# Attention results transposed by VectorE in 32x32 blocks and DMA moves, in place of TensorE's transposes

## The chip, the cores and the metric

One core of a Trainium2 chip runs the whole program. Its engines run side by side, each through its own instruction queue in order: TensorE (PE; its weight loads are listed as PEld), VectorE (DVE), ScalarE (ACT), GpSimd (POOL) and SyncE (SP), which only issues DMAs. They meet through semaphores. The metric is the device time of one launch in microseconds; the difference that a measurement of this kernel can tell is small, since its three runs lie within 0.15 us.

## The reference, cut to what matters

Two layers of a decoder trunk, for 256 tokens of 1024 channels in float32. In each layer a token mixer with three branches (latent attention, a convolution module, a pooling mixer) is merged by gates, and a gated feed-forward network follows. The change touches the attention branch between the weighted values and the output projection:

```
def mla_branch(...):
    ...
    def attend(args):
        qn, qr, start = args
        s = jnp.einsum('bqhd,bkhd->bhqk', qn, k_nope) + jnp.einsum('bqhr,bkr->bhqk', qr, k_rope)
        ...
        p = jax.nn.softmax(s, axis=-1).astype(v.dtype)
        return jnp.einsum('bhqk,bkhd->bqhd', p, v)
    o = lax.map(attend, (qn_blocks, qr_blocks, starts))
    o = o.transpose(1, 0, 2, 3, 4).reshape(B, S, N_HEADS * V_HEAD_DIM)
    return o @ w_o
...
merged = gates[:, :, 0] * y_attn + gates[:, :, 1] * y_conv + gates[:, :, 2] * y_pool
return rms_norm(merged @ w_mix_o, norm_post)
```

Here `o` is 256 tokens by 512 channels (8 heads of 64). For `o @ w_o` TensorE wants `o` with the channels on the partitions: four tiles of 128 channels by 256 tokens.

## The kernel before

**Matrix products in three parts.** Every large product is made of three matmuls: each operand is split into a rounded high part and a low part (the rest), and high x high, high x low and low x high are summed (L460 to L462). Weights stream in as 135 units of 128 x 1024 for each layer. For each unit SP issues the load into a ring of five buffers (L398), ACT makes the high part (`hi`, L861), DVE the low part (`lo`, L1182 where the unit has a scale for its rows, L1186 where not), and TensorE uses it for 12 matmuls of 512 columns. SP may load unit g + 5 when the low part of unit g is done, and ACT makes a high part when TensorE has finished with the unit five earlier. So ACT and DVE work up to four units ahead of TensorE.

**The gate phase.** Units 25 to 48 of a layer (`U_GATE`; here gate 0 to gate 23) are the products for the three sigmoid gates. Between them TensorE does attention, by hand-written order: after gate i, for even i, `after_gate` gives step n = i/2 - 1 of scores, n - 1 of transposed probabilities (P) and n - 2 of weighted values (V). A step is two heads and one half of the tokens, so V0 to V7 follow gates 6 to 20, and V3 completes the first four heads, V7 the last four. ACT and DVE go through the same list with their own parts: while they stand at gate i they split the weights of gate i + 4. In each gate DVE also runs four taps of the convolution (L1261) until all 124 are done, in gate 19.

**The results of attention.** `divide` (L1401) reads V from the PSUM bank and writes the normalised result into `o_sb`. Then, at gates 20 and 22 (`O_AFTER`), `o_transposes` (L748) has TensorE transpose half the channels of `o_sb` each time, four transposes of 128 x 128 through L534 into a `tp` bank (uses O0 and O1 of the bank list `TP`). ACT copies the bank into `hT_hi` (`hi_T`, L895), DVE makes the rest, `hT_lo` (`lo_T`, L1214).

**The convolution's norm** runs beside it, across four engines: the last tap lets GpSimd sum the tiles (L1646 and L1648, the first sum), TensorE forms the mean after gate 22 (L756), DVE centres (L1349), ACT squares (L1024), GpSimd sums again (the second sum), TensorE forms the variance (L782, ahead of unit 51), DVE reads it (`conv_var`, L1357), GpSimd takes the root (L1657), DVE makes a diagonal (L1360), and TensorE spreads it (L788, ahead of unit 52).

**After the gates** come the output projections: pooling (units 49 to 52), attention (`U_ATTNO`, units 53 to 56), convolution (57 to 60). Only the attention units read the transposed results. The bands `sg` and `qk_flat` are reused by several stages: `sg` holds `pooled` until gate 2 and the squares `sq` from gate 23 on.

**A DMA pattern that exists already**: queries, keys and the hidden tiles of the feed-forward network are transposed by DVE in blocks of 32 x 32 (L1321, L1500), and DMAs then carry whole rows of blocks to the right partitions (GpSimd's queue at L1639 and L360, SP's at L360 and L425).

Of the kernel before, what the change touches and what calls it, by code (L numbers as in the profile page):

```python
# [86 lines left out]
def fulls(pair, use):  # L87
# [5 lines left out]
TP = (["X0", "X1", "X2", "X3", "HC0", "HC1", "CQ0", "CQ1", "CKV0", "CKV1",  # L93
       "MT0", "MT1", *(f"{piece}{n}" for n in range(8) for piece in "PV"), "O0", "O1",
       "M0", "M1", "M2", "M3", "F0", "F1", "F2", "F3"])
# [37 lines left out]

O_AFTER = (20, 22)
MT_AFTER, MEAN_AFTER = 2, 22
# [14 lines left out]
def build(nc, W, pool_w, par_d, const_d, gain_d, x_d, xc_d, pos_d, out_d):  # L150
    with ExitStack() as ctx:
# [3 lines left out]
        def sem(name):  # L155
            return ctx.enter_context(nc.semaphore(name))
# [53 lines left out]
        turned_k = [gates[:, 0, D:D + 512], gates[:, 1, D:D + 512], gates[:, 0, D + 512:2 * D]]  # L210
        placed_q = [qk_flat[:, 512 * i:512 * (i + 1)] for i in range(QUADS - 1)] + [gates[:, 1, 512:1024]]
        rope_a, rope_b = hc[:, 0, :], hc[:, 1, :]
        xc = hc[:, :, :].rearrange("p t n -> p (t n)").rearrange("p (c n) -> p c n", c=CT)
# [69 lines left out]
        q_stored = sem("q_stored")  # L283
        k_in = [sem(f"k_in{i}") for i in range(2)]
        conv_dve = sem("conv_dve")
        csum_done = sem("csum_done")
# [20 lines left out]
        def tokens(t):  # L307
            return slice(t * P, (t + 1) * P)
# [44 lines left out]
        def move_keys(eng, l, part):  # L353

            for h in range(2):
                eng.wait_ge(misc_full[h], l * 2 + 1)
            for i in range(HEAD_MOVES // 2 * part, HEAD_MOVES // 2 * (part + 1)):
                c, q = divmod(i, QUADS)
                eng.wait_ge(k_turned, l * (QK // BLK) + c + 1)
                eng.dma_start(u_hc[BLK * c:BLK * (c + 1), q // 2, q % 2, :], turned_k[c][BLK * q:BLK * (q + 1), :]  # L360
                              ).then_inc(k_in[part], 16)

        def hi_stored(eng, l, n):
# [20 lines left out]
        def _(sp):  # L384
# [42 lines left out]
            for l in range(LAYERS):  # L427
                for u in range(0 if l else 1, UNITS):
# [12 lines left out]
                    if u == U_GATE + 5:  # L441
                        move_keys(sp, l, 1)
                    if u == U_CQ:
                        load_gain(l, 0)
# [12 lines left out]
        def _(pe):  # L457
# [23 lines left out]
            for l in range(LAYERS):  # L481
# [265 lines left out]

                def o_transposes(half):  # L748
                    tp_emptied(pe, l, TPN[f"V{4 * half + 3}"])
                    transposes(TPN[f"O{half}"], [(o_sb[:, t, c * P:(c + 1) * P], P)  # L750
                                                 for c in range(2 * half, 2 * half + 2) for t in range(TOK)])

                def norm_mean():
# [5 lines left out]
                def attention(i):  # L759
# [5 lines left out]
                    if v_n is not None:  # L765
                        weighted_values(v_n)
                    if i in O_AFTER:
                        o_transposes(O_AFTER.index(i))
                    if i == MT_AFTER:
# [39 lines left out]
                col_group(U_POOLO + 2, 2, 2, 512, 1, "POOLO", HT, kt0=H_POOL, beside=norm_beside)  # L809
                for half in range(2):  # L810
                    tp_emptied(pe, l, TPN[f"O{half}"])
                col_group(U_ATTNO, 2, 2, 512, 0, "ATTNO", HT, kt0=H_O)
                col_group(U_ATTNO + 2, 2, 2, 512, 1, "ATTNO", HT, kt0=H_O)
# [31 lines left out]
        def _(act):  # L845
# [3 lines left out]
            for l in range(LAYERS):  # L849
# [185 lines left out]
                def store_p(m):  # L1035
# [3 lines left out]
                    if m >= 2:  # L1039
# [3 lines left out]
                                   ACT.Copy).then_inc(tp_free[n % 2], 1)  # L1043

                def exponentials(n):

# [8 lines left out]
                for i in range(GATES):  # L1055
# [20 lines left out]
                    if s_n is not None:  # L1076
                        exponentials(s_n)
                    if i in O_AFTER:
                        half_ = O_AFTER.index(i)
                        hi_T(f"O{half_}", hT_hi[:, H_O + 2 * half_:H_O + 2 * half_ + 2, :])  # L1080
                    if i == MT_AFTER:
                        for h in range(2):
                            hi_T(f"MT{h}", hT_hi[:, H_POOL + 2 * h:H_POOL + 2 * h + 2, :])
                    if i == 18:
                        act.preload_act_table(ACT.Silu)
                his(53, 56)
                conv_silu()
# [59 lines left out]
        def _(dve):  # L1147
# [23 lines left out]
            for l in range(LAYERS):  # L1171
# [223 lines left out]
                def divide(m):  # L1395
# [8 lines left out]
                                      ALU.mult).then_inc(tp_free[n % 2], 1)  # L1404

                for i in range(GATES):
                    s_n, p_n, v_n = after_gate(i)
# [4 lines left out]
                    if v_n is not None:  # L1412
                        divide(v_n)
                    if i == MEAN_AFTER + 1:
                        conv_centre()
                    lo(U_GATE + 4 + i)
                    if i == MT_AFTER:
                        for h in range(2):
                            k = slice(H_POOL + 2 * h, H_POOL + 2 * h + 2)
                            lo_T(f"MT{h}", hT_lo[:, k, :], hT_hi[:, k, :])  # L1420
                    if i in O_AFTER:
                        half_ = O_AFTER.index(i)
                        k = slice(H_O + 2 * half_, H_O + 2 * half_ + 2)
                        lo_T(f"O{half_}", hT_lo[:, k, :], hT_hi[:, k, :])
                    taps(4)
# [22 lines left out]

                los(53, 54)
                conv_var()  # L1450
                los(54, 55)
# [99 lines left out]
        def _(pool):  # L1551
# [30 lines left out]
            for l in range(LAYERS):  # L1582
# [54 lines left out]
                for c in range(QK // BLK):  # L1637
                    for q in range(QUADS):
                        pool.dma_start(placed_q[q][BLK * c:BLK * (c + 1), :], turned_q[c][BLK * q:BLK * (q + 1), :]  # L1639
                                       ).then_inc(q_in, 16)  # L1640
                move_keys(pool, l, 0)

                def tile_sum(src, which):
# [7 lines left out]
                pool.wait_ge(conv_dve, (l + 1) * len(TAP_ORDER))  # L1651
                tile_sum(cacc, 0)
                pool.wait_ge(sq_done, l + 1)
                pool.wait_ge(csum_done, l * 4 + 2)
# [131 lines left out]
```

## Time and profile before

| | us |
|---|---|
| median of 3 runs | 787.54 (787.43 to 787.58) |
| the profiled execution, its own time | 787.39 |
| its span, first to last instruction | 785.6 |
| TensorE busy | 777.3 (99%) |
| VectorE busy | 573.2 (73%) |
| ScalarE busy | 421.9 (54%) |
| GpSimd busy | 96.6 (12%) |

The busy share is an average. A matmul's duration is longer than the distance to the next one, since matmuls are pipelined: the 512-column ones take 0.39 us each and start 0.23 us apart. What a piece of TensorE's work costs is therefore read from starts, not from durations.

### The profile page before, as it was taken

How to read it: one execution, taken by the hardware profiler on the slowest of the kernel's cores; microseconds unless marked ns; L12 is line 12 of the kernel's file. 1: busy time of each engine (PE TensorE's matmuls, PEld its weight loads, DVE VectorE, ACT ScalarE, POOL GpSimd, SP SyncE). 2: the span in 40 equal slices, each digit the busy share in tenths (PEclk: the TensorE clock that was granted, in tenths of full speed). 3: DMA queues.
4: the chain of work that ended last, by engine and by line, in shares of the span. 5: the costliest groups of instructions: out<-in, count | busy, mean ns of one | idle time of the engine just before them, and what ended most of it. 6: DMA issues, size and time to landing. Idle time of an engine off the chain costs nothing.

```text
span 785.6 us, 10199 instructions
## 1 busy us (share of the span) xinstructions
PE 777.3 (99%) x3708; PEld 656.6 (84%) x3708; DVE 573.2 (73%) x826; ACT 421.9 (54%) x596; POOL 96.6 (12%) x147
## 2 busy tenths in 40 slices
PE   8999999999999999999999999999999999999997
PEld 7898888888888888888889888888888888888885
DVE  6689999789675666654476999996887665556553
ACT  6577555564554454454475656565546554445441
POOL 1624000122300000000221230002303000000000
PEclk9999999999999999999999999999999999999999
DMA  9677544545566666676365684444564666666631
GB/s 358 227 251 212 185 159 153 176 153 181 179 238 220 207 212 223 212 241 204 129 203 173 217 253 146 161 161 160 166 219 153 243 212 214 215 219 208 227 137 53
DMA packets 53456, 154.39 MB, mean 197 GB/s; under 512 B 10544, under 2 KB 15664, under 8 KB 53408
## 3 DMA queue, kind: packets, MB, share of 16 engines
q1 hardware_dynamic: 51856, 149.72, 57.3%
q0 software_dynamic: 1408, 3.52, 1.6%
q8 instruction: 29, 0.48, 0.3%
q10 hardware_dynamic: 144, 0.52, 0.2%
q14 instruction: 19, 0.16, 0.1%
HBM read 143.77 MB, written 1.05 MB: 184 GB/s over the span
## 4 chain that ended last, share of the span: by engine, by line
PE 98%; DMA 1%; ACT 0%; DVE 0%; DVEq 0%; POOLq 0%; issue 0%; POOL 0%; ACTq 0%
PE acc L460 28%; PE acc L462 28%; PE acc L461 28%; PE acc L579 7%; PE tp L534 2%; PE misc L725 1%; PE tp L743 1%; PE tp L546 1%; DMA gates<-x_cols 1%; PE misc L692 0%; PE tp L707 0%; PE misc L462 0%; PE misc L461 0%; PE misc L460 0%; PE misc L694 0%; ACT xT_hi L888 0%
## 5 line engine op out<-in xcount | busy, mean ns | idle before, releaser
L1186 DVE TENSOR_TENSOR w_lo<-raw,w_hi 128x1024 fp32r<-128x1024 f32 (+2 forms) x246 | 298.7, 1226 | 123.0 <-ACT w_hi L861 122.5
L861 ACT ACTIVATE w_hi<-raw 128x1024 fp32r<-128x1024 f32 (+2 forms) x252 | 258.1, 1039 | 163.2 <-PE acc L462 159.2
L460 PE MATMUL acc<-w_hi,xT_hi 128*128 128x512 f32 (+2 forms) x692 | 267.9, 387 | 0.0
L462 PE MATMUL acc<-w_hi,xT_lo 128*128 128x512 f32 (+2 forms) x692 | 264.9, 383 | 0.0
L461 PE MATMUL acc<-w_lo,xT_hi 128*128 128x512 f32 (+2 forms) x692 | 264.6, 382 | 0.0
L462 PEld LDWEIGHTS acc<-w_hi,xT_lo 128*128 128x128 f32 x692 | 129.9, 188 | 24.9
L461 PEld LDWEIGHTS acc<-w_lo,xT_hi 128*128 128x128 f32 x692 | 130.0, 188 | 24.0
L460 PEld LDWEIGHTS acc<-w_hi,xT_hi 128*128 128x128 f32 x692 | 130.0, 188 | 23.7
L460 PE MATMUL acc<-w_hi,hT_hi 128*128 128x512 f32 (+1 forms) x300 | 117.2, 391 | 0.0
L462 PE MATMUL acc<-w_hi,hT_lo 128*128 128x512 f32 (+1 forms) x300 | 116.2, 387 | 0.0
L461 PE MATMUL acc<-w_lo,hT_hi 128*128 128x512 f32 (+1 forms) x300 | 116.1, 387 | 0.0
L1261 DVE SCALAR_TENSOR_TENSOR cacc<-hcT,par,cacc 128x256 f32<-128x256 f32 x240 | 101.0, 479 | 0.0
L462 PEld LDWEIGHTS acc<-w_hi,hT_lo 128*128 128x128 f32 x300 | 56.3, 188 | 11.4
L461 PEld LDWEIGHTS acc<-w_lo,hT_hi 128*128 128x128 f32 x300 | 56.3, 188 | 11.1
L460 PEld LDWEIGHTS acc<-w_hi,hT_hi 128*128 128x128 f32 x300 | 56.3, 188 | 10.9
L1590 POOL TENSOR_SCALAR mean<-ssq 128x1 f32<-128x1 f32 x23 | 9.7, 422 | 442.9 <-ACT qk L880 442.4
L1050 ACT ACTIVATE qk<-misc,nmx 128x128 f32<-128x128 f32 (+1 forms) x32 | 13.2, 416 | 42.8 <-DVE nmx L1387 42.8
L1182 DVE SCALAR_TENSOR_TENSOR w_lo<-raw,par,w_hi 128x512 fp32r<-128x512 f32 (+1 forms) x30 | 25.4, 878 | 6.2 <-ACT w_hi L861 6.1
L1162 DVE TENSOR_TENSOR acc<-acc,gain 128x512 f32<-128x512 f32 x16 | 10.4, 691 | 25.6 <-ACT qk L880 22.6
L1507 DVE TENSOR_TENSOR hT_lo<-gates,hT_hi 128x512 fp32r<-128x512 f32 (+1 forms) x24 | 14.4, 639 | 20.1 <-ACT hT_hi L1102 20.1
L1102 ACT ACTIVATE hT_hi<-gates 128x512 fp32r<-128x512 f32 (+1 forms) x24 | 12.9, 586 | 24.9 <-DMA gates<-gates 24.8
L579 PE MATMUL acc<-w_hi,xT_hi 128*128 128x512 f32 x76 | 24.0, 396 | 1.5 <-ACT w_hi L861 1.5
(148 smaller groups left out, 640.9 us busy)
## 6 DMA issues: line engine op xcount, KB each, us to landing
raw<-weights SPq DMA_DIRECT2D x247, 512.0 KB, 3.8
raw<-weights SPq DMA_DIRECT2D x14, 384.0 KB, 3.4
gates<-gates SPq DMA_DIRECT2D x160, 32.0 KB, 2.5
raw<-weights SPq DMA_DIRECT2D x8, 288.0 KB, 3.7
gain<-gains SPq DMA_DIRECT2D x4, 512.0 KB, 7.0
qk<-gates POOLq DMA_DIRECT2D x18, 64.0 KB, 3.4
x_sb<-x_rows SPq DMA_DIRECT2D x2, 512.0 KB, 9.4
out_rows<-x_sb SPq DMA_DIRECT2D x4, 256.0 KB, 2.0
```

The lines of the kernel that those rows point to most:

```text
L460: pe.matmul(out, a_hi, b_hi, start=start, stop=False)
L461: pe.matmul(out, a_hi, b_lo, start=False, stop=False)
L462: return pe.matmul(out, a_lo, b_hi, start=False, stop=stop)
L534: mm = pe.transpose(tp[0:rows, b, i * P:(i + 1) * P], src, ident)
L579: mm = pe.matmul(b, src[:, kt, tokens(t)], w[:, s, 512 * j:512 * (j + 1)], start=kt == 0 and src is xT_hi and w is w_hi, stop=last and kt ...
L861: ins = act.activation(w_hi[:, s, first:end], raw[:, s, first:end], ACT.Copy, scale=by)
L1050: e = act.activation(probs[:, n % 2, i, 0:keys], misc[:, n % 2, i * keys:(i + 1) * keys], ACT.Exp, bias=nmx[:, n % 2, i:i + 1], accum_out= ...
L1102: act.activation(hid_part(hT_hi, j, t), placed_for(j, t), ACT.Copy).then_inc(hid_hi, 1)
L1182: ins = dve.scalar_tensor_tensor(out=w_lo[:, s, first:end], in0=raw[:, s, first:end], scalar=par[:, l, col:col + 1], in1=f(w_hi[:, s, firs ...
L1186: ins = dve.tensor_tensor(w_lo[:, s, 0:width], raw[:, s, 0:width], f(w_hi[:, s, 0:width]), ALU.subtract)
L1261: ins = dve.scalar_tensor_tensor(out=cacc[:, c, :], in0=src, scalar=w, in1=cacc[:, c, :], op0=ALU.mult, op1=ALU.add)
L1507: dve.tensor_tensor(hid_part(hT_lo, j, t), placed_for(j, t), f(hid_part(hT_hi, j, t)), ALU.subtract).then_inc(hid_lo, 1)
```

## The change

The two uses O0 and O1 of the transpose banks are gone, and with them four transposes each. In their place, for each half of the channels:

1. **DVE** turns the half in 32 x 32 blocks, two instructions of 128 x 256 (`turn_o`), after it has divided V3 (gate 12) and V7 (gate 20).
2. **DMAs** place the blocks, 16 for each half, each 32 partitions of 512 bytes (`move_o`). Half 0 goes by GpSimd's queue, behind the keys and ahead of the first sum. Of half 1, eight go by GpSimd's queue, between its first and its second sum, and eight by SP's, four behind the load of unit 54 and four behind the load of unit 55.
3. **ACT** makes the high part in two instructions of 128 x 256 (`hi_o`): of half 0 at gate 18, of half 1 behind the high part of unit 53.
4. **DVE** makes the low part likewise (`lo_o`): of half 0 at gate 18, of half 1 behind the low part of unit 53 and ahead of `conv_var`.
5. **TensorE** waits for the low parts ahead of units 53 and 54.

Half 0 lies in `sg`, half 1 in `qk_flat`.

```
-O_AFTER = (20, 22)
+O_TURNED, O_PARTS = (3, 7), 18
...
+        turned_o = sg[:, 0, :], qk_flat[:, 1024:1536]
+        placed_o = sg[:, 1, :], qk_flat[:, 0:512]
...
+        def move_o(eng, l, half, which, first, last):
+            eng.wait_ge(o_turned, TOK * (2 * l + half + 1))
+            for i in range(first, last):
+                a, q = divmod(i, QUADS)
+                eng.dma_start(placed_o[half][BLK * q:BLK * (q + 1), P * a:P * (a + 1)],
+                              turned_o[half][BLK * a:BLK * (a + 1), P * q:P * (q + 1)]).then_inc(o_in[which], 16)
...
+                    if U_ATTNO < u < U_ATTNO + 3:
+                        i = 8 + 4 * (u - U_ATTNO - 1)
+                        move_o(sp, l, 1, 1, i, i + 4)
...
-                def o_transposes(half):
-                    tp_emptied(pe, l, TPN[f"V{4 * half + 3}"])
-                    transposes(TPN[f"O{half}"], [(o_sb[:, t, c * P:(c + 1) * P], P)
-                                                 for c in range(2 * half, 2 * half + 2) for t in range(TOK)])
...
-                    if i in O_AFTER:
-                        o_transposes(O_AFTER.index(i))
...
-                for half in range(2):
-                    tp_emptied(pe, l, TPN[f"O{half}"])
-                col_group(U_ATTNO, 2, 2, 512, 0, "ATTNO", HT, kt0=H_O)
+                def results_ready(i):
+                    pe.wait_ge(o_lo, TOK * (2 * l + i + 1))
+                col_group(U_ATTNO, 2, 2, 512, 0, "ATTNO", HT, kt0=H_O, beside=results_ready)
...
+                def hi_o(half):
+                    o_landed(act, l, half)
+                    for t in range(TOK):
+                        act.activation(o_part(hT_hi, half, t), o_placed(half, t), ACT.Copy).then_inc(o_hi, 1)
...
-                his(53, 56)
+                his(53, 54)
+                hi_o(1)
+                his(54, 56)
...
+                def turn_o(half):
+                    tp_emptied(dve, l, TPN[f"V{O_TURNED[half]}"])
+                    v = o_sb[:, :, 2 * P * half:2 * P * (half + 1)]
+                    for t in range(TOK):
+                        dve.transpose(o_blocks(turned_o[half])[:, :, t, :, :].rearrange("p q k j -> p k q j"),
+                                      v[:, t, :].rearrange("p (k q j) -> p k q j", k=2, q=QUADS)
+                                      ).then_inc(o_turned, 1)
...
+                    if v_n in O_TURNED:
+                        turn_o(O_TURNED.index(v_n))
...
                 los(53, 54)
+                lo_o(1)
                 conv_var()
...
+                move_o(pool, l, 0, 0, 0, QUADS * QUADS)
...
                 tile_sum(cacc, 0)
+                move_o(pool, l, 1, 0, 0, QUADS * QUADS // 2)
                 pool.wait_ge(sq_done, l + 1)
```

How the instructions stand on TensorE around the end of gate 20, before (L743 is V7, L534 the transposes of O0, L460 the first matmul of gate 21):

```order
L462 MATMUL acc<-w_hi,xT_lo 128x512
L743 MATMUL tp<-v_sb,qk 128x64 [waits tp_free1,tp_free0]
L743 MATMUL tp<-v_sb,qk 128x64 x3
L534 MATMUL tp<-const,qk 128x128 [waits tp_free0,tp_free1]
L534 MATMUL tp<-const,qk 128x128 x3
L460 MATMUL acc<-w_hi,xT_hi 128x512 [waits lo_done]
```

and now (L780 is V7):

```order
L499 MATMUL acc<-w_hi,xT_lo 128x512
L780 MATMUL tp<-v_sb,qk 128x64 [waits tp_free1,tp_free0]
L780 MATMUL tp<-v_sb,qk 128x64 x3
L497 MATMUL acc<-w_hi,xT_hi 128x512 [waits lo_done]
L498 MATMUL acc<-w_lo,xT_hi 128x512
```

Between V7 and the next gate nothing is left. After gate 22 the same happens ahead of the convolution's mean.

GpSimd's queue between the keys and the root of the variance, before:

```order
L360 DMA u_hc<-gates 32x512 [waits k_turned] x5
L1646 TENSOR_TENSOR u_hc<-cacc 128x512 [waits conv_dve]
L1648 TENSOR_TENSOR u_hc<-u_hc 128x256 [waits csum_done]
L1646 TENSOR_TENSOR u_hc<-sg 128x512 [waits csum_done,sq_done]
L1648 TENSOR_TENSOR u_hc<-u_hc 128x256 [waits csum_done]
L1657 TENSOR_TENSOR crstd<-cvar,half 128x2 [waits var_in]
```

and now:

```order
L369 DMA u_hc<-gates 32x512 [waits k_turned] x5
L387 DMA sg<-sg 32x128 [waits o_turned]
L387 DMA sg<-sg 32x128 x15
L1702 TENSOR_TENSOR u_hc<-cacc 128x512 [waits conv_dve]
L1704 TENSOR_TENSOR u_hc<-u_hc 128x256 [waits csum_done]
L387 DMA qk<-qk 32x128 [waits o_turned]
L387 DMA qk<-qk 32x128 x7
L1702 TENSOR_TENSOR u_hc<-sg 128x512 [waits csum_done,sq_done]
L1704 TENSOR_TENSOR u_hc<-u_hc 128x256 [waits csum_done]
L1714 TENSOR_TENSOR crstd<-cvar,half 128x2 [waits var_in]
```

Eight DMAs stand now between the two sums, and sixteen ahead of the first.

VectorE from gate 19 on to `conv_var`, before (L1401 divides V7; the `hT_lo<-tp` rows are the low parts of O0 and O1):

```order
L1186 TENSOR_TENSOR w_lo<-raw,w_hi 128x1024 [waits hi_done]
L1261 SCALAR_TENSOR_TENSOR cacc<-hcT,par,cacc 128x256 [waits conv_dve] x3
L1401 TENSOR_TENSOR qk<-tp,rinv 128x128 [waits inv_done,tp_full1]
L1182 SCALAR_TENSOR_TENSOR w_lo<-raw,par,w_hi 128x512 [waits hi_done]
L1182 SCALAR_TENSOR_TENSOR w_lo<-raw,par,w_hi 128x512
L1214 TENSOR_TENSOR hT_lo<-tp,hT_hi 128x512 [waits tp_hi]
...
L1214 TENSOR_TENSOR hT_lo<-tp,hT_hi 128x512 [waits tp_hi]
L1349 TENSOR_TENSOR u_hc<-cacc,misc 128x1024 [waits misc_full0]
...
L1186 TENSOR_TENSOR w_lo<-raw,w_hi 128x1024 [waits hi_done]
L1357 TENSOR_SCALAR cvar<-misc 128x2 [waits misc_full1]
```

and now, from the low part of unit 47 at gate 18 on:

```order
L1224 TENSOR_TENSOR w_lo<-raw,w_hi 128x1024 [waits hi_done]
L1457 TENSOR_TENSOR hT_lo<-sg,hT_hi 128x2x128 [waits o_hi] x2
...
L1439 TENSOR_TENSOR qk<-tp,rinv 128x128 [waits inv_done,tp_full1]
L1449 STREAM_TRANSPOSE qk<-qk 128x2x4x32 [waits tp_free1]
L1449 STREAM_TRANSPOSE qk<-qk 128x2x4x32
...
L1387 TENSOR_TENSOR u_hc<-cacc,misc 128x1024 [waits misc_full0]
...
L1224 TENSOR_TENSOR w_lo<-raw,w_hi 128x1024 [waits hi_done]
L1457 TENSOR_TENSOR hT_lo<-qk,hT_hi 128x2x128 [waits o_hi] x2
L1395 TENSOR_SCALAR cvar<-misc 128x2 [waits misc_full1]
```

The low parts of half 1 now stand directly ahead of the variance's reader.

## Rows read from the trace of the kernel before

**Rows 1.** The page: busy time, share, instructions; the last chain by engine; TensorE's longest wait

```profile
PE 777.3 (99%) x3708; PEld 656.6 (84%) x3708; DVE 573.2 (73%) x826; ACT 421.9 (54%) x596; POOL 96.6 (12%) x147
PE 98%; DMA 1%; ACT 0%; DVE 0%; DVEq 0%; POOLq 0%; issue 0%; POOL 0%; ACTq 0%
...
PE acc L579 <- ACT w_hi L861: 1.5, 1, 1.5
```

**Rows 2.** Busy time of each engine in a window of the gate phase (us, instructions)

```profile
110.00:150.00 40.00, 40.00 (x218) 34.35 (x217) 39.40 (x80) 24.24 (x45) 2.34 (x2) 1.00 0.51 163
```

**Rows 3.** Timeline of PE after gates 16, 20, 22: start, us, instruction, count

```profile
131.84 1.00 PE L743 MATMUL tp<-v_sb,qk 128*128 128x64 f32 x8
132.65 0.47 PE L460 MATMUL acc<-w_hi,xT_hi 128*128 128x512 f32 x1
...
144.59 1.00 PE L743 MATMUL tp<-v_sb,qk 128*128 128x64 f32 x8
145.43 0.60 PE L534 MATMUL tp<-const,qk 128*128 128x128 f32 x4
145.79 0.48 PE L460 MATMUL acc<-w_hi,xT_hi 128*128 128x512 f32 x1
...
151.35 0.60 PE L534 MATMUL tp<-const,qk 128*128 128x128 f32 x4
151.79 0.60 PE L756 MATMUL misc<-u_hc,const 128*128 128x256 f32 x2
```

**Rows 4.** PE on the transpose banks from `qk`: min/median/max ns

```profile
L534 PE MATMUL tp<-const,qk x64: 271/272/329, 89.5 to 537.9; 128*128 128x128 f32 x64
```

**Rows 5.** Block transposes, low parts and high parts on DVE and ACT: min/median/max ns, forms

```profile
L1500 DVE STREAM_TRANSPOSE gates<-u_hc x24: 400/672/707, 236.9 to 730.9; 128x512 f32<-128x512 f32 x20, 128x256 f32<-128x256 f32 x4
...
L1214 DVE TENSOR_TENSOR hT_lo<-tp,hT_hi x16: 415/618/692, 44.3 to 538.8; 128x512 fp32r<-128x512 f32 x8, 128x384 fp32r<-128x384 f32 x4, 128x256 fp32r<-128x256 f32 x4
...
L895 ACT ACTIVATE hT_hi<-tp x16: 379/542/606, 43.8 to 538.2; 128x512 fp32r<-128x512 f32 x8, 128x384 fp32r<-128x384 f32 x4, 128x256 fp32r<-128x256 f32 x4
```

**Rows 6.** Timeline of DVE, gate 19 to the diagonal [idle before <-releaser]

```profile
143.89 1.28 DVE L1261 SCALAR_TENSOR_TENSOR cacc<-hcT,par,cacc 128x256 f32<-128x256 f32 x3
145.63 0.29 DVE L1401 TENSOR_TENSOR qk<-tp,rinv 128x128 f32<-128x128 f32 x1 [0.47 <-PE tp L743]
145.84 2.38 DVE L1182 SCALAR_TENSOR_TENSOR w_lo<-raw,par,w_hi 128x512 fp32r<-128x512 f32 x2
...
148.74 2.93 DVE L1182 SCALAR_TENSOR_TENSOR w_lo<-raw,par,w_hi 128x512 fp32r<-128x512 f32 x4
152.62 0.69 DVE L1214 TENSOR_TENSOR hT_lo<-tp,hT_hi 128x512 fp32r<-128x512 f32 x1 [0.94 <-ACT hT_hi L895]
...
160.93 0.16 DVE L1357 TENSOR_SCALAR cvar<-misc 128x2 f32<-128x2 f32 x1 [0.77 <-PE misc L782]
161.93 0.48 DVE L1360 TENSOR_SCALAR diag<-const,crstd 128x128 f32<-128x128 f32 x2 [0.83 <-POOL crstd L1657]
```

**Rows 7.** Timeline of ACT: the squares, and the high parts of units 53 and 54

```profile
154.53 1.06 ACT L1024 ACTIVATE sg<-u_hc 128x1024 f32<-128x1024 f32 x1 [1.94 <-DVEq L1352]
...
157.86 2.00 ACT L861 ACTIVATE w_hi<-raw 128x1024 fp32r<-128x1024 f32 x2
```

**Rows 8.** DMAs of GpSimd's queue, then SP's: issue ns and landing us, min/median/max

```profile
L1639 POOL DMA_DIRECT2D qk<-gates x18: 496/498/629, 64.8 to 455.0; - x18
...
DMA to landing us min/median/max: 1.9/3.5/5.7
...
L425 SPq DMA_DIRECT2D gates<-gates x192: 507/591/1485, 239.7 to 745.8; - x192
...
DMA to landing us min/median/max: 1.8/2.5/3.7
```

**Rows 9.** Timeline of GpSimd: end of the first sum, start of the second

```profile
146.61 1.07 POOL L1648 TENSOR_TENSOR u_hc<-u_hc 128x256 f32<-128x256 f32 x1
155.66 1.29 POOL L1646 TENSOR_TENSOR u_hc<-sg 128x512 f32<-128x512 f32 x1 [7.99 <-ACT sg L1024]
```

**Rows 10.** Timeline of PE: the spread ahead of unit 52

```profile
163.61 0.59 PE L788 MATMUL misc<-diag,const 128*128 128x256 f32 x2
```

More of the change, by code:

```diff
@@ L93 @@
 TP = (["X0", "X1", "X2", "X3", "HC0", "HC1", "CQ0", "CQ1", "CKV0", "CKV1",
-       "MT0", "MT1", *(f"{piece}{n}" for n in range(8) for piece in "PV"), "O0", "O1",
+       "MT0", "MT1", *(f"{piece}{n}" for n in range(8) for piece in "PV"),
        "M0", "M1", "M2", "M3", "F0", "F1", "F2", "F3"])
@@ L284, in build @@
         k_in = [sem(f"k_in{i}") for i in range(2)]
+        o_turned = sem("o_turned")
+        o_in = [sem(f"o_in{i}") for i in range(2)]
+        o_hi = sem("o_hi")
+        o_lo = sem("o_lo")
         conv_dve = sem("conv_dve")
@@ L361, in move_keys, with o_blocks, o_part, o_placed @@
                               ).then_inc(k_in[part], 16)
+        def o_blocks(buf):
+            return buf.rearrange("p (q t k j) -> p q t k j", q=QUADS, t=TOK, k=2)
+        def o_part(dst, half, t):
+            k = slice(H_O + 2 * half, H_O + 2 * half + 2)
+            return dst[:, k, tokens(t)].rearrange("p k (q j) -> p k q j", q=QUADS)
+        def o_placed(half, t):
+            return o_blocks(placed_o[half])[:, :, t, :, :].rearrange("p q k j -> p k q j")
+        def move_o(eng, l, half, which, first, last):
[4 more added lines that the diff above has]
+                              turned_o[half][BLK * a:BLK * (a + 1), P * q:P * (q + 1)]).then_inc(o_in[which], 16)
+        def o_landed(eng, l, half):
+            moves = QUADS * QUADS
+            eng.wait_ge(o_in[0], 16 * moves * (3 * l + (2 if half == 0 else 3)) // 2)
+            if half:
+                eng.wait_ge(o_in[1], 16 * moves * (l + 1) // 2)
         def hi_stored(eng, l, n):
@@ L1077, in _ @@
                         exponentials(s_n)
-                    if i in O_AFTER:
-                        half_ = O_AFTER.index(i)
-                        hi_T(f"O{half_}", hT_hi[:, H_O + 2 * half_:H_O + 2 * half_ + 2, :])
+                    if i == O_PARTS:
+                        hi_o(0)
                     if i == MT_AFTER:
@@ L1404, in divide, with lo_o @@
                                       ALU.mult).then_inc(tp_free[n % 2], 1)
+                def turn_o(half):
[5 more added lines that the diff above has]
+                                      ).then_inc(o_turned, 1)
+                def lo_o(half):
+                    for t in range(TOK):
+                        dve.wait_ge(o_hi, TOK * (2 * l + half) + t + 1)
+                        dve.tensor_tensor(o_part(hT_lo, half, t), o_placed(half, t), f(o_part(hT_hi, half, t)),
+                                          ALU.subtract).then_inc(o_lo, 1)
                 for i in range(GATES):
@@ L1420, in _ @@
                             lo_T(f"MT{h}", hT_lo[:, k, :], hT_hi[:, k, :])
[L1421 to L1424, printed above, removed]
+                    if i == O_PARTS:
+                        lo_o(0)
                     taps(4)
```

## The prediction, blind

> **What bounds the kernel now.** I read the page's busy times and the last chain first, then TensorE's waits, then the gate phase. TensorE is busy for 777.3 of 785.6 us and makes 98% of the last chain; in the whole span its longest wait is 1.5 us, at the start [rows 1]. So the time is the sum of what TensorE does, and an instruction taken from it shortens the span by its share of the stream, as long as nobody else becomes late. The nearest to that is VectorE: 39.40 us of a 40 us window in the gate phase [rows 2], which the change loads further. All times below are of layer 0; layer 1 runs the same code and gets the same price. The profiled execution took 787.39 us, 0.15 below the median of 787.54; I subtract from the median.
>
> **What it removes.** Four times four transposes. What they cost is read from starts, with a neighbour of the same shape. After gate 16, where no O stands, V starts at 131.84 and the next gate's first matmul at 132.65: 0.81. After gate 20 the same eight pieces start at 144.59 and the matmul at 145.79: 1.20. O0 costs 0.39. O1 starts at 151.35 and the mean's matmul behind it at 151.79: 0.44, and without O1 the mean would follow the last gate matmul directly, as O1 does now [rows 3]. A layer saves 0.83, two save 1.66 us.
>
> The duration of such a transpose in the trace is 0.27 us [rows 4], but the next starts after 0.11 (0.44 / 4). The Trainium skill (TensorE: Matmul & The Clock Gate, Part 4: PE-mode transpose) gives about 275 ns for a 128x128 transpose within a kernel. That agrees with the duration; taken as the price it would make the saving 16 x 0.275 = 4.4 us, an estimate from the page.
>
> **What it adds on VectorE.** Block transposes of 128x256: nothing of that form runs in this stage; the feed-forward part has it, and the minimum of its group is 0.40. The bounds are 0.34 (half of the 0.67 of a 128x512) and 0.67; I take 0.40, which is the form itself. Two of them, overlapping a little, and the wait for the divide's own end: 0.75 a half. Low parts of 128x256: 0.42 as the minimum of their group (read from PSUM there, from SBUF here; 0.69, the price of twice the size, bounds it), two 0.75. The low parts removed were 0.69 each [rows 5]. Up to the centring at about 153.2 VectorE gains 3 x 0.75 = 2.25 and loses two times some 0.6 (0.69 less the overlap with the next). Two idle stretches cover the rest: 0.47 before the divide of V7 and 0.94 before the low part of O1, which waited for ScalarE [rows 6]. 2.25 - 1.2 - 1.41 = -0.36: the centring comes no later, rather some 0.4 earlier. In between it is late: at gate 19 by 1.5, so the last tap ends at 145.17 + 1.5 = 146.7 instead of 145.17. Weights do not suffer: the low part of unit 49 ended at 148.2, and would now end at about 150.0 (below); TensorE reaches unit 49 after the mean (151.79) and gate 23 (12 matmuls of 0.23, 2.75), at 154.8 before, 154 now.
>
> **On ScalarE.** Two copies of 0.38 a half [rows 5] in place of one of 0.60. Half 0 falls in gate 18, before an idle stretch. Half 1 follows the high part of unit 53, which ends at about 158.9 [rows 7]. Behind the copies are the high parts of 54 and 55. TensorE begins unit 51 behind the variance, which released `conv_var` at 160.93 [rows 6], and a unit takes 2.75, so it wants 54 at 169. Free.
>
> **On GpSimd.** Sixteen DMAs of half 0 at gate 12: at 0.50 each [rows 8] 8 us. VectorE passes gate 12 seven gates of 3.2 us (12.75 for four, by rows 3) ahead of 145.2, at about 122; the last move goes out at 130 and lands by 136, and the copy stands at gate 18, near 139. The queue is then empty until the first sum. Free. The first sum ended 2.5 after the last tap (147.68 against 145.17) [rows 6, 9], so it now ends at 149.2, and the mean's matmul starts at 151.79 - 0.83 = 150.96 at the earliest: 1.7 in hand. Eight DMAs follow, 4.0 us, to 153.2; the second sum waits for the squares, to 155.66 before [rows 9] and about 155.3 now. Free by 2 us.
>
> **The rule against it.** The issues at L1639 took 0.50 (at most 0.63) beside a VectorE that was busy throughout [rows 8]. The Trainium skill (SBUF — State Buffer, Who interferes with whom) says that GpSimd's descriptor writing is blocked while VectorE runs in a two-port mode. The trace shows no such wait beside the same low parts and taps. What a blocked queue would do here is rival 3; the sum goes by the row.
>
> **On SP's queue, and when half 1 lands.** The block transposes of half 1 end at about 147.8 (146.7, divide 0.3, 0.75). Beside the first sum the two scaled low parts of unit 49 took 2.38 where four others took 2.93 [rows 6]; they now run 147.8 to 150.0. Then SP may load unit 54, issues four moves of 0.59 (to 152.7), loads 55, issues the last four: the last goes out at 155.0. Landing 2.5 (1.8 to 3.7) [rows 8]: 157.5, at most 158.7. GpSimd's last goes out at 152.7 and lands by 156.2 (at most 158.4). ScalarE gets there at 158.5 to 158.9, so it waits for nothing. The load of unit 55 goes out some 2.5 us later than before, that of 56 some 4; ScalarE took 55 at some 160.7 at the earliest (its buffer frees when TensorE ends unit 50) and 56 later. Free.
>
> **The tightest place** is VectorE behind the low part of unit 53. It was through at 160.16 (0.77 idle, then `conv_var` at 160.93). The low parts of half 1 fill that gap. From `conv_var` to the diagonal it takes 1.48 (160.93 to 162.41) [rows 6], and TensorE wants the diagonal at 163.61 - 0.83, less 0.2 for its weight load: 162.6 [rows 10]. So `conv_var` must start by 161.1. With everything as before it starts at 160.16 + 0.75 = 160.9; with the earlier centring at about 160.5. Free by 0.2 to 0.6. Read backwards, half 1 must have landed by 161.1 - 2 x 0.38 - 0.42 = 159.9; I have 157.5.
>
> **The sum:** -1.66, nothing on the path: 787.54 - 1.66 = **785.9 us**.
>
> **The rivals.**
> 1. *Small stalls* (20%). The margin of 0.2 to 0.6 at the diagonal, or the 1.7 at the mean, is used up: contention like that of the slowed low parts of unit 49 (about 1 us in 2.4), or moves that land at 160 to 161. It speaks for it that VectorE is full; against it that each engine in the chain has idle time there. A stall of 0.2 to 0.8 a layer gives 786.3 to 787.5, within 0.2% of before.
> 2. *Half 1 lands late* (5%), the slower side. SP's issues reach 1.49 instead of 0.59 [rows 8]. At 1.1 each, the last one goes out at 150.3 + 4.4 + 0.6 + 3.3 = 158.6 and lands at 161.1 to 162.3; ScalarE, the low parts, `conv_var` and the diagonal are all behind it. Each us past 159.9 is a us of TensorE, in each layer. At 162.3 that is 2.4 a layer: 787.54 - 1.66 + 4.8 = 790.7. It breaks even at 160.7 and is slower by 0.2% from 161.5. The median issue and the windows before it speak against it.
> 3. *GpSimd's issues are held up by VectorE* (2%), slower too. If each lasts as long as a scaled low part, 1.19 (half of 2.38) [rows 6], the eight take 9.5 and end at 158.7; the second sum ends at 161.2, and the moves land at 162.2. TensorE wants the second sum for its variance some 0.5 before `conv_var`'s 160.93, less 0.83: at 159.6. The landing weighs more: 162.2 - 159.9 = 2.3 a layer, 787.54 - 1.66 + 4.6 = 790.5. This is what the Trainium skill's rule above would give.
> 4. *A transpose is worth its duration* (3%): 16 x 0.27 = 4.3 us, 783.2. The starts in the timeline speak against it. The Trainium skill's page on TensorE, named above, would give this.
>
> **How the numbers follow.** Forecast 70%, small stalls 20%, late landing 5%, GpSimd held up 2%, more gain 3%. What a measurement can tell from no change is about 0.2%, 1.57 us, so the threshold lies at 785.97, just above my 785.88. That is close: of the 70% I give 50 to faster (the two readings of 0.39 and 0.44 are each good to some 0.02, the runs to 0.08) and 20 to same. Faster 0.53, same 0.40, slower 0.07. The range: from 785.4 (0.44 saved at all four places, and some 0.1 more at each from the slower start of the first matmul behind small ones) to 787.3 (rival 1 nearly whole); the cases beyond, 10% together, are left out, and so is the last part of rival 1.
>
> **What the new profile would show.** TensorE instructions 16 fewer and its busy time some 1.7 us less; V7 followed by a gate matmul after 0.81; the mean's matmul 0.23 behind the last gate matmul. GpSimd's second sum still released by ScalarE's squares, not by its own queue. ScalarE's copies of half 1 behind a high part with no idle before them; if they wait for a DMA, by how much. `conv_var` at about 160.5, released by VectorE's own work rather than by TensorE. Wrong it would be with any wait of TensorE at the mean, the spread, or units 53 and 54: the first two are in the chain through VectorE, the last two have some 5 us in hand (160.5 against 166.6 - 0.8).

## The result and the profile after

The changed kernel is slower: 789.61 us (789.28 to 790.0, nine runs) against 787.5 us (787.41 to 787.76, nine runs), 1.0028 times the time before, with a 95% interval of 1.002 to 1.0036. The forecast was 785.9 us, the range 785.4 to 787.3. The profiled execution took 789.28 us with a span of 787.4, 1.8 more than before.

Everything in the body of the kernel went as forecast. Busy times and the last chain, on the page of the kernel after:

```profile
PE 775.1 (98%) x3692; PEld 654.6 (83%) x3692; DVE 575.7 (73%) x838; ACT 421.7 (54%) x600; POOL 120.0 (15%) x195
PE 98%; DMA 1%; ACT 0%; DVE 0%; DVEq 0%; POOLq 0%; issue 0%; POOL 0%; ACTq 0%
```

Against [rows 1], TensorE has 16 instructions fewer and is busy 2.2 us less, while the span is longer. TensorE's timeline of the kernel after (start, duration, instruction, count) answers to [rows 3]:

```profile
144.42 1.00 PE L780 MATMUL tp<-v_sb,qk 128*128 128x64 f32 x8
145.22 0.48 PE L497 MATMUL acc<-w_hi,xT_hi 128*128 128x512 f32 x1
...
150.56 0.39 PE L499 MATMUL acc<-w_hi,xT_lo 128*128 128x512 f32 x1
150.78 0.59 PE L788 MATMUL misc<-u_hc,const 128*128 128x256 f32 x2
```

V7 is followed by a gate matmul after 0.80 (1.20 before), and the mean's matmul comes 0.22 behind the last gate matmul. The same instruction, before and after, moves like this: 145.79 to 145.22 behind the place of O0, 151.79 to 150.78 behind that of O1, and the last matmul of the program starts at 779.53 before and 777.72 after. Of these last 1.81 us, 0.17 came from the start of the kernel, where TensorE waited for its first weights; the four places gave 0.39, 0.44, 0.39 and 0.44, each read from the instructions on either side of it, together 1.65 before rounding. So TensorE finished 1.8 us earlier and the program ended 1.8 us later. The loss of 3.6 us lies wholly behind the last matmul.

What stands there is not on the page: instructions of each engine's sequencer (the rows with a q behind the engine's name, which wait, branch and issue) are not counted as busy. The rows of the program's closing line (L151 before, L152 after; engine, operation, count: min/median/max ns, first and last start in us), first of the kernel before:

```profile
L151 PEldq DRAIN  x1: 4267/4267/4267, 775.7 to 775.7; - x1
L151 ACTq DRAIN  x1: 672/672/672, 780.1 to 780.1; - x1
L151 POOLq DRAIN  x1: 3937/3937/3937, 781.1 to 781.1; - x1
L151 DVEq DRAIN  x1: 1449/1449/1449, 781.7 to 781.7; - x1
...
L151 SPq DRAIN  x1: 7/7/7, 785.4 to 785.4; - x1
```

and of the kernel after:

```profile
L152 POOLq EVENT_SEMAPHORE  x2: 17/17/17, 787.2 to 787.3; - x2
...
L152 ACTq DRAIN  x1: 672/672/672, 778.3 to 778.3; - x1
L152 POOLq DRAIN  x1: 7857/7857/7857, 779.3 to 779.3; - x1
L152 DVEq DRAIN  x1: 1447/1447/1447, 779.9 to 779.9; - x1
...
L152 SPq DRAIN  x1: 7/7/7, 783.6 to 783.6; - x1
```

Each engine ends with a DRAIN and then meets the others at a barrier (the semaphore events of the same line), and the span ends there. The row of a DRAIN begins while the engine's own last work still runs, so its duration holds the rest of that work too. The timeline of the kernel before has the last instructions of ScalarE and GpSimd:

```profile
780.51 0.19 ACT L1142 ACTIVATION_READ_ACCUMULATOR qk<-acc 128x1 f32 x1
...
781.12 0.55 POOL L1681 TENSOR_TENSOR rstd<-mean,half 128x1 f32<-128x1 f32 x1
```

ScalarE's last instruction ends at 780.70 and its DRAIN at 780.74: 0.04 us are its own, of 0.67. VectorE's outlasts its last instruction by 0.05. GpSimd's last instruction ends at 781.67 and its DRAIN 3.35 us later. Only GpSimd's DRAIN takes long by itself. Its row begins, in both kernels, 4.1 us before the output has landed. Before, this DRAIN ended at 785.03 and SP, which waits for the output's store, reached its own at 785.36: the store set the end, with 0.33 us to spare. After, SP got there at 783.6, and GpSimd's DRAIN, twice as long (7.86 against 3.94), ended at 787.13. Everyone waited for it; in the waits of SP in the kernel after (engine and line, who it waited for: us in total, times, longest):

```profile
SPq L152 <- PEq L152: 3.8, 1, 3.8
```

The releaser is an inferred one: TensorE had been at the barrier since 778, and the last to arrive was GpSimd, whose semaphore events stand at 787.2. The chain of waits (start, duration, engine) doesn't show it either. Its last rows in the kernel after:

```profile
778.21 0.60 ACT qk L1180
779.27 0.60 POOLq L152
779.89 0.75 DVE x_sb L1206
780.64 0.66 DVEq L152
```

It ends at 781.3, in a span of 787.4. In the kernel before it ended at 783.1 of 785.6, with this row:

```profile
782.46 0.66 DVEq L151
```

Nothing in the chain's shares says what fills the 6.1 us behind it in the kernel after.

What did the change add there? GpSimd's groups of the kernel after (busy us, mean ns of one | idle before):

```profile
L387 POOL DMA_DIRECT2D sg<-sg x32 | 15.6, 497 | 95.2 <-DVE sg L1449 95.2
L1694 POOL DMA_DIRECT2D qk<-gates x18 | 9.1, 510 | 19.6 <-DVE gates L1359 19.6
L387 POOL DMA_DIRECT2D qk<-qk x16 | 7.9, 498 | 0.0
L369 POOL DMA_DIRECT2D u_hc<-gates x12 | 5.9, 496 | 1.9 <-DVE gates L1359 1.9
L1694 POOL DMA_DIRECT2D gates<-gates x6 | 3.0, 497 | 0.0
```

With four loads of constants that is 88 DMAs on GpSimd's queue; before there were 40, without the two groups of L387. Both numbers give the DRAIN the same way, and that became the theory.

### The profile page after: what moved, and what is told of

It is laid out like the page before. It is cut to its first block, busy times and chain, and to the rows that moved or that the text cites. A ratio compares the mean times of both kernels' runs of the same rounds, so it can differ in the third digit from the quotient of the medians.

```text
span 787.4 us, 10245 instructions
## 1 busy us (share of the span) xinstructions
PE 775.1 (98%) x3692; PEld 654.6 (83%) x3692; DVE 575.7 (73%) x838; ACT 421.7 (54%) x600; POOL 120.0 (15%) x195
## 4 chain that ended last, share of the span: by engine, by line
PE 98%; DMA 1%; ACT 0%; DVE 0%; DVEq 0%; POOLq 0%; issue 0%; POOL 0%; ACTq 0%
PE acc L497 28%; PE acc L499 28%; PE acc L498 28%; PE acc L616 7%; PE tp L571 2%; PE misc L762 1%; PE tp L780 1%; PE tp L583 1%; DMA gates<-x_cols 1%; PE misc L729 0%; PE tp L744 0%; PE misc L499 0%; PE misc L498 0%; PE misc L497 0%; PE misc L731 0%; ACT xT_hi L919 0%
## 5 line engine op out<-in xcount | busy, mean ns | idle before, releaser
L387 POOL DMA_DIRECT2D sg<-sg x32 | 15.6, 497 | 95.2 <-DVE sg L1449 95.2
```

Of the source, the lines that this page charges most:

```text
L387: eng.dma_start(placed_o[half][BLK * q:BLK * (q + 1), P * a:P * (a + 1)], turned_o[half][BLK * a:BLK * (a + 1), P * q:P * (q + 1)]).then_i ...
```

## The experiments

**Theory:** GpSimd's DRAIN takes a fixed time and some 0.08 us more for each DMA that has gone out on its queue; (7.857 - 3.937) / 48 = 0.082. The change put 48 there. **Rivals:** the DRAIN waits for the bytes of the moves, or it grows with the work of GpSimd or with the place of the DMAs; or the loss is one of the late half that the prediction had weighed, and the DRAIN only looks long because others are late.

**1. The kernel before with 48 idle DMAs more.** What they move is read by nobody. Two waves of twelve a layer, behind the moves of the keys:

```diff
+                pool.wait_ge(late_in, 16)
+                for wave in range(2 * l, 2 * (l + 1)):
+                    if wave:
+                        pool.wait_ge(extra_in, 16 * 12 * wave)
+                    for i in range(12):
+                        k, q = divmod(i, QUADS)
+                        pool.dma_start(scratch[BLK * q:BLK * q + BLK, P * k:P * k + P],
+                                       const[BLK * q:BLK * q + BLK, K_ONE:K_ONE + P]).then_inc(extra_in, 16)
```

Ahead of its last norm GpSimd waits until all 48 have landed, which they had long before (the last at 477 us).

> The kernel before with 48 more DMAs on GpSimd's queue (24 a layer, 16 KB each, 32 partitions of 512 bytes, from a constant to scratch, behind the keys, in two waves a layer; GpSimd has nothing else to do there), nothing else changed; the output is the same. Theory A (GpSimd's closing DRAIN grows with the DMAs that its queue carried: 3.94 us with 40 of them, 7.86 with 88, so 0.67 + 0.082 each): DRAIN 7.86, span 789.2, time 791.1, that is 3.6 above before. Theory B (the long DRAIN belongs to something else in the changed kernel: where the moves stand, what they wait for, the transposes): DRAIN 3.94, time 787.5.

Measured: 790.98 us against 787.31, 1.0045 [1.0032, 1.0059]. The DRAIN, and SP's wait at the end, in this kernel:

```profile
L151 POOLq DRAIN  x1: 7859/7859/7859, 780.9 to 780.9; - x1
```
```profile
SPq L151 <- PEq L151: 3.8, 1, 3.8
```

The kernel before, with nothing of the change but the number of DMAs, has the DRAIN of the kernel after to 2 ns, and loses 3.7 us. All transposes are still on TensorE. What the change does in the gate phase is not needed for the loss.

**2. The same 48 with 4 bytes each** (`+ 1` in place of `+ BLK` and `+ P` in both slices).

> The same 48 DMAs more, but each carries one partition of 4 bytes instead of 16 KB. If the DRAIN pays for each DMA: 7.86, time 791.1. If it pays for bytes or for rows of partitions moved (32 in each before, 1 now): near 3.9 to 4.1, time 787.5.

Measured: 790.95 us, 1.0045 [1.0031, 1.0059], the DRAIN again 7859 ns. Neither bytes nor rows matter: 16 KB in 32 partitions and 4 bytes in one cost the same. This rival falls.

**3. Half as many** (one wave a layer, 24 in all).

> The kernel before with 24 DMAs more instead of 48. Under the theory the closing DRAIN is 0.67 + 64 x 0.082 = 5.90 us, 1.96 longer; it ended 0.33 before SP's last wait, so the time grows by 1.6: 789.0. If the cost is a step (above some number of DMAs), 787.4 or 791.

Measured: 789.16 us against 787.52, 1.002 [1.0011, 1.0029].

```profile
L151 POOLq DRAIN  x1: 5896/5896/5896, 781.2 to 781.2; - x1
```
```profile
SPq L151 <- PEq L151: 1.8, 1, 1.8
```

24 DMAs more than before: 3.937 + 24 x 0.0817 = 5.90. The DRAIN is linear in the number; the time lost is that less the 0.33 by which the store came later before: 1.96 - 0.33 = 1.63 (measured 1.64) for 24, 3.92 - 0.33 = 3.59 (measured 3.67) for 48.

**4. The kernel after with a DRAIN of its own in each layer**, behind GpSimd's part of a normalization, where it has nothing urgent to do:

```diff
                 norm(R_F + 1)
+                pool.drain()
```

(`pool.drain()` writes one DRAIN into GpSimd's queue.)

> The changed kernel with one DRAIN instruction more on GpSimd's queue in each layer, behind its last norm, where the engine then has nothing to do for over 100 us. If a DRAIN pays for the DMAs since the last one: the two in the middle take 3.6 to 4.3 us, hidden, the closing one about 0.7, time 785.8. If it pays for all that the queue ever carried: the closing one stays at 7.86 and the time at 789.6.

Measured: 786.05 us against 787.31, 0.9984 [0.9975, 0.9993]; span 784.0 (one of the eleven runs took 787.52, the others 785.69 to 786.20). The new DRAINs, and the closing one:

```profile
L1729 POOLq DRAIN  x2: 4101/4268/4436, 221.8 to 607.1; - x2
```
```profile
L152 POOLq DRAIN  x1: 664/664/664, 779.5 to 779.5; - x1
```

The 7.2 us are paid in the middle, where nobody waits for GpSimd, and the closing one is down to 0.66. The same change of the gate phase that lost 2 us now gains 1.3. The price is paid once for each DMA, at the next DRAIN: 46 stand ahead of the first (4.436) and 42 between it and the second (4.101).

**5. The DRAIN in layer 0 alone** (`if l == 0:` ahead of it).

> The changed kernel with the DRAIN in layer 0 alone. If a DRAIN pays for the DMAs since the last one: the closing one pays for layer 1's 42, 4.10 us, begins at about 779.4 and ends at 783.5, just when the last store has landed: 785.9. If one DRAIN in the program is enough whatever comes later: closing one 0.7, the same time. If DRAINs do not settle anything: 7.86, 789.6.

Measured: 786.12 us against 787.52, 0.9983 [0.9974, 0.9992]. Closing DRAIN:

```profile
L152 POOLq DRAIN  x1: 4094/4094/4094, 779.6 to 779.6; - x1
```

It ends at 783.69. The store landed at about the same time, and SP reached its own DRAIN at 783.9, so GpSimd's costs nothing. This is the state of the kernel before, at 42 DMAs instead of 40: a DRAIN that just fits behind the store.

**6 and 7. The controls: the same DRAIN in the kernel before, and in the one with 48 more.**

> The kernel before with the same two DRAINs on GpSimd's queue. In the kernel before the closing DRAIN (3.94 us) ended at 785.03 and the last store's landing, which SP waits for, at 785.36. So under the theory (a DRAIN pays 0.67 + 0.082 for each DMA since the last) the closing one falls to 0.7 and the time stays: 787.4, within 0.1. If the DRAINs help in another way, about 1 us or more faster, as the changed kernel's 1.3 below before might also suggest.

> The kernel before with the 48 DMAs more on GpSimd's queue and the two DRAINs. Under the theory all of the 3.6 us that the 48 DMAs cost is gone: 787.4. If the DMAs themselves cost something beside the DRAIN (their descriptors, their traffic): what is left above 787.4.

Measured: 787.50 us (0.9999 [0.999, 1.0008]) and 787.51 us (1.0 [0.9991, 1.0009]) against 787.52. The DRAINs of the layers, in the kernel before and in the one with 48 more:

```profile
L1672 POOLq DRAIN  x2: 2141/2306/2472, 222.7 to 608.8; - x2
```
```profile
L1682 POOLq DRAIN  x2: 4099/4266/4432, 222.5 to 608.7; - x2
```

In both kernels the closing DRAIN is down to 662 ns. A DRAIN gives the kernel before nothing, because there the store ended later anyway. It takes back the whole loss of the 48 idle DMAs. So the DRAIN isn't a gain of its own that flatters experiment 4, and 48 idle DMAs cost nothing but their share of it.

**8. The change with all its moves off GpSimd's queue.** SP issues half 0, four moves behind each of four loads; of half 1 ScalarE issues eight at gate 21 and SP eight as before:

```diff
-                move_o(pool, l, 0, 0, 0, QUADS * QUADS)
...
-                move_o(pool, l, 1, 0, 0, QUADS * QUADS // 2)
...
+                    if U_GATE + 21 < u < U_GATE + 26:
+                        i = 4 * (u - U_GATE - 22)
+                        move_o(sp, l, 0, 0, i, i + 4)
...
+                    if i == 21:
+                        move_o(act, l, 1, 0, 0, QUADS * QUADS // 2)
```

> The changed kernel with its moves off GpSimd's queue: half 0 by SP's, four behind each load of units 47 to 50, eight of half 1 by ScalarE's at gate 21, the other eight by SP's as they are. GpSimd's queue is back at 40 DMAs. Theory A: DRAIN 3.94, span 783.8, time 785.8 (the forecast's 1.66 us, unhidden). Theory B (the gain is lost for another reason): 789.6 still. If the later loads on SP's queue or ScalarE's issues cost TensorE something, between 785.8 and 787.5, and TensorE shows a wait.

Measured: 789.96 us against 787.31, 1.0033 [1.002, 1.0045]. The closing DRAIN is back at 3939 ns, but TensorE ended late: its last matmul starts at 781.69 instead of 777.72. ScalarE's timeline in the gate phase:

```profile
147.83 5.17 ACTq L387 DMA_DIRECT2D qk<-qk  x8
153.10 1.34 ACT L895 ACTIVATE w_hi<-raw,par 128x512 fp32r<-128x512 f32 x2 [5.15 <-issue]
```

VectorE's, behind it:

```profile
154.48 1.41 DVE L1225 SCALAR_TENSOR_TENSOR w_lo<-raw,par,w_hi 128x512 fp32r<-128x512 f32 x2 [3.30 <-ACT w_hi L895]
155.81 1.21 DVE L1392 TENSOR_TENSOR u_hc<-cacc,misc 128x1024 f32<-128x1024 f32 x1
```

and TensorE's, behind that:

```profile
160.84 0.61 PE L815 MATMUL misc<-const,u_hc 128*128 128x1 f32 x4 [0.96 <-POOL u_hc L1708]
...
164.87 0.70 PE L821 MATMUL misc<-diag,const 128*128 128x256 f32 x2 [0.54 <-DVE diag L1403]
```

Eight issues of 0.60 to 0.69 us stood ahead of the high part of unit 51 on ScalarE's queue. It started at 153.10 instead of 148.32, VectorE waited 3.3 us for it before its low part, the centring started at 155.81 instead of 152.09, and TensorE waited at the variance and at the spread. This is the price of a wrong place in the order, and it is the mechanism of my rivals 1 and 2 made real: what comes late in this chain stops TensorE. The expectation failed: of its three cases the time alone fits theory B (789.6), though the DRAIN is as theory A had it and TensorE's own end is 4.0 us later. I had looked only for the issues' cover and not for what is queued behind them. That these issues are the cause, and not SP's sixteen further moves, experiment 9 has to show.

**9. The same, with ScalarE's eight at gate 22**, behind that high part (`i == 22`).

> As the kernel without GpSimd moves, but ScalarE issues its eight one gate later, behind the high part of unit 51 instead of ahead of it. If its 789.96 came from the 5.2 us of issues standing ahead of that high part (VectorE's low part of unit 51 and with it the centring were late by 3.7): the high part and the centring are back in time (152.1), the issues end at about 154.9 instead, the squares come 1.5 late and conv_var at about 161.3, 0.2 to 0.4 later than TensorE allows: about 786.4, GpSimd's closing DRAIN 3.94. If it came from SP's sixteen moves among the loads: still near 789.9.

Measured: 785.93 us against 787.43, 0.9979 [0.997, 0.9988]; span 784.3, DRAIN 3937 ns, no wait of TensorE in the gate phase. The rows of ScalarE, and of VectorE's centring:

```profile
149.61 0.71 ACT L895 ACTIVATE w_hi<-raw,par 128x512 fp32r<-128x512 f32 x1
149.66 4.58 ACTq L387 DMA_DIRECT2D qk<-qk  x7
```
```profile
153.05 1.21 DVE L1392 TENSOR_TENSOR u_hc<-cacc,misc 128x1024 f32<-128x1024 f32 x1
```

One gate later the same eight issues are free: seven of them go out behind both high parts of that unit, while ScalarE has nothing to do until the squares at 154.35. The centring is 1 us later than in the kernel after and still in time. SP's moves are where they were in experiment 8, so they didn't cost its 4 us. The time is 0.5 better than expected: the issues ended at 154.2 instead of 154.9, and `conv_var` started at 160.61 instead of 161.3, so the small wait at the spread that I had expected did not occur.

**10. And with the variance ahead of the low parts of half 1 on VectorE** (`conv_var()`, then `lo_o(1)`).

> The same with conv_var ahead of the two low parts of half 1 on VectorE. If the low parts are what brings conv_var past its limit: the wait at the spread is gone and the time is 785.9. If it is the late high part of unit 53 alone: no difference from the kernel beside it.

Measured: 785.97 us, 0.9981 [0.9973, 0.999], the same as experiment 9. The question was about a wait at the spread that experiment 9 turned out not to have, so equal times were to be expected. `conv_var` starts at 160.32 instead of 160.61, but TensorE, which it waits for, is earlier by as much. It starts 0.53 to 0.54 behind TensorE's variance matmul in the kernels before and after and in experiments 9 and 10 alike:

```profile
160.32 0.16 DVE L1400 TENSOR_SCALAR cvar<-misc 128x2 f32<-128x2 f32 x1 [0.81 <-PE misc L815]
```

The low parts ahead of it, which the prediction called the tightest place, cost nothing.

**The DRAIN in all kernels.** 0.66 us and 0.0818 us for each DMA of the queue since the DRAIN before. Of the 0.66, 0.58 to 0.59 is the rest of GpSimd's instruction ahead of the DRAIN, the same short statistic in every kernel; counted from that instruction's end the DRAIN takes 0.08 + 0.0818 n.

| DMAs since the last DRAIN | measured, us | 0.66 + 0.0818 n |
|---|---|---|
| 0 | 0.662, 0.664 | 0.66 |
| 18 | 2.141 | 2.13 |
| 22 | 2.472 | 2.46 |
| 40 | 3.937, 3.939 | 3.93 |
| 42 | 4.094 to 4.101 | 4.10 |
| 46 | 4.432 to 4.436 | 4.42 |
| 64 | 5.896 | 5.90 |
| 88 | 7.857, 7.859 | 7.86 |

The best kernels, 9, 10, 4 and 5 at 785.93, 785.97, 786.05 and 786.12 us, beat both the kernel before and the one after. Their order among themselves is within the spread of their runs.

## Why the prediction was wrong

**What bounds the kernel: wrong in one sentence.** "So the time is the sum of what TensorE does" held up to 779.5 us of the span before, and the 6.1 us behind it were counted as constant. They were a race of two branches, the output's store and GpSimd's DRAIN, 0.33 us apart. This is the step that failed, with the term that it put at nothing: what a DMA on GpSimd's queue costs behind its issue. The trace of the kernel before had the rows (shown above): a chain that ends 2.5 us before the span does, and a DRAIN that outlasts its engine's own work by 3.35 us where ScalarE's does by 0.04. The prediction's sign of being wrong was a wait of TensorE at the mean, the spread, or units 53 and 54: none came, and the time was wrong all the same.

**On GpSimd: wrong.** I wrote "Sixteen DMAs of half 0 ... 8 us ... Free" and costed each DMA by its issue. The issue was right and hidden. The 0.082 us that each leaves behind for the DRAIN were not counted. By the prediction's own method the sum would be: DRAIN 781.09 - 1.66 = 779.43, plus 3.94 + 48 x 0.082 = 7.87, gives 787.30, against 785.36 for SP before: 1.94 us slower, 789.5. Measured: 789.61.

**What it removes: right.** 0.39 and 0.44 a layer, 1.66 in all; measured 0.39, 0.44, 0.39, 0.44, in all 1.65. With the DRAIN out of the way (experiments 4, 5, 9, 10) the kernels took 785.93 to 786.12, against a forecast of 785.9. Against the runs beside them these kernels are 1.26 to 1.50 us faster, not 1.66. The missing part is not at the four places: they give 1.65 or 1.66 in the trace of each of these kernels. It lies in TensorE's first wait for weights, behind which the stream stands 0.17 us earlier than before in the kernel after and 0.10, 0.13, 0.48 and 0.19 later in experiments 4, 5, 9 and 10, and in the time outside the span (1.8 before, 1.9 to 2.05 in these). The start moved by as much (0.30 later) in the control of experiment 6, where TensorE's work is unchanged; why it moves is open.

**VectorE, ScalarE, SP: right.** In VectorE's timeline after, to be read beside [rows 6]:

```profile
146.68 0.77 DVE L1449 STREAM_TRANSPOSE qk<-qk 128x256 f32<-128x256 f32 x2
147.38 4.79 DVE L1220 SCALAR_TENSOR_TENSOR w_lo<-raw,par,w_hi 128x512 fp32r<-128x512 f32 x6
152.09 1.21 DVE L1387 TENSOR_TENSOR u_hc<-cacc,misc 128x1024 f32<-128x1024 f32 x1
...
158.95 0.75 DVE L1457 TENSOR_TENSOR hT_lo<-qk,hT_hi 128x256 fp32r<-128x256 f32 x2
159.96 0.16 DVE L1395 TENSOR_SCALAR cvar<-misc 128x2 f32<-128x2 f32 x1 [0.25 <-PE misc L812]
```

The pairs took 0.77 and 0.75, forecast 0.75 each. The centring started at 152.09, about 1 us earlier than the 153.2 of before, where I had said 0.4. `conv_var` started at 159.96 instead of the 160.5 forecast, and it still waited 0.25 us for TensorE, where I had it released by VectorE's own work; so VectorE had more in hand than I gave it. ScalarE's two copies stand right behind a high part, with no idle time, so half 1 had landed (its last block at 157.1, forecast 157.5):

```profile
156.72 1.05 ACT L892 ACTIVATE w_hi<-raw 128x1024 fp32r<-128x1024 f32 x1
157.67 0.71 ACT L1080 ACTIVATE hT_hi<-qk 128x256 fp32r<-128x256 f32 x2
```

SP's last group of moves ended at 155.7 (forecast 155.0), and landing took 1.6 to 3.7 us (forecast 1.8 to 3.7).

**The second sum: right.** GpSimd's timeline after answers to [rows 9]:

```profile
147.89 1.08 POOL L1704 TENSOR_TENSOR u_hc<-u_hc 128x256 f32<-128x256 f32 x1
148.92 3.93 POOL L387 DMA_DIRECT2D qk<-qk  x8
154.53 1.29 POOL L1702 TENSOR_TENSOR u_hc<-sg 128x512 f32<-128x512 f32 x1 [1.69 <-ACT sg L1055]
```

The sum is released by the squares, with 1.69 us in hand where the prediction had 2.

**The rivals.** Rival 1 (small stalls, 20%) didn't occur: TensorE's longest wait after is still the one at the start, 1.8 us. Rival 2 (half 1 late) and its price of 790.7 are near the measured time by accident; its mechanism was absent. Experiment 8 shows what such lateness is worth when it is there: about 3.7 us over two layers (the last matmul is 2.15 later than before, the four places had saved 1.65, and 0.1 came from the start). Rival 3 (GpSimd's issues held up by VectorE) is refuted by the row above, eight issues in 3.93 us, at most 0.514 us each. The rule of the Trainium skill behind it (SBUF — State Buffer, Who interferes with whom) speaks of VectorE in a two-port mode and did not show itself here. No row shows whether any VectorE instruction beside the issues was in such a mode, so the rule itself is not tested. Rival 4 fell too: each transpose was worth 0.10 (1.65 / 16), not 0.27. Nothing among the 7% for "slower" was what happened; the right mechanism had no chance of its own, and the range (785.4 to 787.3) could not hold 789.6.

The Trainium skill (VectorE: DVE Perf Modes, The DRAIN you can't avoid) says that the DRAINs before and behind a program take a constant of about 12 ns on all five engines. The trace agrees for part of them: at the start of these kernels the DRAINs of four engines took 7 to 10 ns, and SP's 7 at the end. GpSimd's took 167 to 169 ns at the start, and at the end the others took 0.66 us or more. Most of that is the rest of the engine's own work: about 35 ns of ScalarE's 672 to 676, and 52 of VectorE's 1447 to 1449, come behind it. GpSimd's is not constant at all: 77 ns behind its own work with no DMA since the last DRAIN, 7274 with 88. There the measurement decides.

## What to carry to other kernels

Before moving DMAs to GpSimd's queue, look at the last microseconds of the trace of before: compare the end of the chain with the end of the span, read each engine's DRAIN, and count 0.082 us for each DMA added to that queue, against whatever else ends last. Where the DRAIN would end last, either put one in the middle of the program, where GpSimd is idle, or give the moves to another queue, at a place behind the last instruction there that somebody waits for. And a body that is limited by one engine throughout says nothing about what ends the program: TensorE's stream got 1.8 us shorter here, while the whole got 2 us longer.

## What the runs showed of the hardware

GpSimd's DRAIN lasts 0.08 us behind the engine's own last instruction (0.66 in its row) and 0.0818 us more for each DMA issued on its queue since its last DRAIN. That holds whether the DMA moved 16 KB or 4 bytes, and although all of them had landed long before (in the kernel after the last by 540 us, and the closing DRAIN begins at 779). What it does in that time no row shows. ScalarE's DRAIN doesn't grow: 0.672 to 0.676 us with one DMA on its queue, 0.674 with 17; and SP's took 7 ns behind 489 to 537 DMAs. An issue of one of the moves cost 0.50 us on GpSimd, 0.59 on SP and 0.61 on ScalarE (medians).
